# One encoder kernel, one VectorE split moved behind two later steps in the odd layer's head loop

## The reference, cut to what matters

```python
s = einsum('bqhgd,bkhd->bhgqk', qx, kx) * scale     # 128 queries x up to 384 keys
s = where(valid, s, -inf)
m = maximum(max(s), sink)
p = exp(s - m);  p = p / (sum(p) + exp(sink - m))
o = einsum('bhgqk,bkhd->bqhgd', p, vx)
x = x + (o * silu(gate)) @ w_out
```

## Time and profile before

| what | value |
|---|---|
| time, median of 3 runs | 1117.99 us (1117.44 to 1118.64) |
| the profiled execution, its own time | 1119.73 us |
| its span, first to last instruction | 1118.0 us |
| mean granted TensorE clock | 0.994 of full speed |
| PE busy | 1093.4 us, 98% |
| PE weight loads busy | 913.1 us, 82% |
| DVE busy | 967.5 us, 87% |
| ACT busy | 678.7 us, 61% |

### The profile page before, as it was taken

The page is one execution under the profiler, slowest core; times in us unless marked ns, Lnnn a source line. Parts: engine busy times, 40 slices in busy tenths (PEclk is TensorE's granted clock), DMA queues, the critical chain, the costliest instruction groups (busy, mean ns, idle before and its releaser), DMA issues. The chain is left out here.

```text
span 1118.0 us, 18504 instructions
## 1 busy us (share of the span) xinstructions
PE 1093.4 (98%) x5690; PEld 913.1 (82%) x5690; DVE 967.5 (87%) x1956; ACT 678.7 (61%) x1310; POOL 0.2 (0%) x4
## 2 busy tenths in 40 slices
PE   8999999999999999999999999999999999999996
PEld 7778878888888888888888867878888888888876
DVE  6879989889889889889889888888888888988886
ACT  6475665654654654654654765367677666677764
POOL 0000000000000000000000000000000000000000
PEclk9999999999999999999999999999999999999998
DMA  7614423324224224225125120563332324323111
GB/s 231 167 41 106 140 76 93 96 75 101 87 75 114 74 75 125 62 75 140 47 75 150 44 71 22 124 160 97 98 94 56 94 63 121 100 75 94 57 39 76
DMA packets 132634, 103.67 MB, mean 93 GB/s; under 512 B 5488, under 2 KB 118512, under 8 KB 132592
## 3 DMA queue, kind: packets, MB, share of 16 engines
q1 hardware_dynamic: 131760, 102.28, 33.4%
q10 hardware_dynamic: 832, 0.85, 0.2%
HBM read 77.95 MB, written 2.10 MB: 72 GB/s over the span
## 5 line engine op out<-in xcount | busy, mean ns | idle before, releaser
L75 PE MATMUL bank_proj<-hH,w_hi 128*128 128x512 f32 x856 | 341.4, 399 | 1.1 <-DVE w_lo L1323 1.1
L77 PE MATMUL bank_proj<-hH,w_lo 128*128 128x512 f32 x856 | 334.4, 391 | 0.0
L76 PE MATMUL bank_proj<-hL,w_hi 128*128 128x512 f32 x856 | 334.3, 391 | 0.0
L77 PEld LDWEIGHTS bank_proj<-hH,w_lo 128*128 128x128 f32 x856 | 160.8, 188 | 34.9
L75 PEld LDWEIGHTS bank_proj<-hH,w_hi 128*128 128x128 f32 x856 | 161.2, 188 | 32.2 <-DVE w_lo L1323 2.0
L76 PEld LDWEIGHTS bank_proj<-hL,w_hi 128*128 128x128 f32 x856 | 161.2, 188 | 29.8 <-issue 0.2
L2087 ACT ACTIVATE probs<-probs,small 128x256 f32<-128x256 f32 (+1 forms) x128 | 70.9, 556 | 55.2 <-DVE small L2355 54.8
L1323 DVE TENSOR_TENSOR w_lo<-w_raw,w_hi 128x1024 fp32r<-128x1024 f32 x73 | 88.3, 1218 | 0.9 <-ACT w_hi L789 0.9
L2094 ACT ACTIVATE probsT<-bank_odd_turn 128x256 fp32r<-128x256 f32 (+1 forms) x128 | 49.0, 434 | 64.4 <-PE bank_odd_turn L1810 63.7
L789 ACT ACTIVATE w_hi<-w_raw 128x1024 fp32r<-128x1024 f32 x73 | 76.9, 1053 | 0.2
L918 ACT ACTIVATE scaled<-decay 128x1024 f32<-128x1024 f32 x32 | 34.0, 1062 | 61.8 <-PE bank_score L611 59.7
(11 more groups left out here) (463 smaller groups left out, 2157.8 us busy)
## 6 DMA issues: line engine op xcount, KB each, us to landing
w_raw<-in_w_in_even SPq DMA_DIRECT2D x71, 512.0 KB, 4.7
w_raw<-in_w_in_odd SPq DMA_DIRECT2D x36, 512.0 KB, 4.9
qs<-parts SPq DMA_DIRECT2D x96, 128.0 KB, 2.4
ks<-parts SPq DMA_DIRECT2D x40, 256.0 KB, 4.5
o_raw<-in_w_out_even SPq DMA_DIRECT2D x15, 512.0 KB, 6.3
o_raw<-in_w_out_odd SPq DMA_DIRECT2D x14, 512.0 KB, 6.7
mixT<-in_x SPq DMA_DIRECT2D x4, 256.0 KB, 6.0
rope<-in_rope SPq DMA_DIRECT2D x2, 512.0 KB, 7.5
```

The lines of the kernel that those rows point to most:

```text
L75: pe.matmul(out, hi, moving_hi, start=start, stop=False)
L76: pe.matmul(out, hi, moving_lo, start=False, stop=False)
L77: return pe.matmul(out, lo, moving_hi, start=False, stop=stop)
```

## The change

In half 0 of rounds 1 to 7, the split of the next queries (`part(h, 1)`) no longer follows the rotation. The low part of y, the low part of the second transposed block and the maxima of the third block come first, and the split after them. Half 1 keeps its order, and round 0 is as it was. No instruction is added or removed.

```diff
                 if not zeroth:
                     rotate(h, 2 * half + 1)
-                    part(h, 2 * half + 1)
                 if not half and not first:
                     low_y(h - 1, 1)
+                if half:
+                    part(h, 3)
                 low_turn(h, half, 1)
                 maxima(h, half, 2)
+                if not half and not first:
+                    part(h, 1)
                 if first:
                     low(0, 2)
                     part(0, 0)
```

## The result

The changed kernel takes 1119.12 us (median of 21 runs) beside 1116.90 us of the kernel before, timed with it. The medians differ by 2.2 us; the ratio is 1.0015 with a 95% interval of 1.0009 to 1.0021, which is 1.7 us slower, between 1.0 and 2.3. That is less than the 0.2% that the prediction took for the least that can be told from no change, yet the interval excludes 1. The forecast was 1.74 us slower, 1119.7 us by the median of 3 runs shown ahead (1117.99).

What follows compares the result with a forecast made beforehand. TensorE, busy 344.0 of 348 us in the odd layer's loop, was taken as the bound; 0.84 us for six rounds plus 0.90 for round 7 gave +1.74 on 1117.99, 1119.7 us, with a range of 1118.9 to 1120.2 us.

Steps and rivals of the forecast that it cites:

- y's part moves up, the wait goes: Half 0: y's low part starts 0.60 us after the rotation's last addition started; TensorE's 0.32 us wait before `out_tile` 0 goes.
- `low_turn(1)` is held by ScalarE's copy: Half 0, VectorE: `low_turn(1)` starts 1.05 us after `turns(1)`, gaining only 0.40 us, after some 0.8 us idle.
- The split is 1.07 us long and 0.53 us of it are hidden: After the maxima, the split delays VectorE by 1.07 us; the gap before the swapped halves hides 0.53; `low_turn(2)` 0.14 later.
- The upper bound of 1.25 us: The split's longest cost in its new place, both durations end to end plus a 0.13 us gap; +1.3 us over seven rounds.
- Given back at `values(2)`, and 0.14 us on top: Rounds 1 to 6, half 0: TensorE loses the 0.32 us won at `out_tile` 0 plus 0.14 a round, 0.84 us together.
- Round 7 without a gap: Round 7: no idle time hides the split; 1.07 less 0.17 us makes `values(2)` and the tail 0.90 us later.
- The queue costs nothing: SyncE's DMAs behind the split go 3.3 us later, yet queries and weight loads still arrive in time; cost nothing.
- The rival in which the weights come late: Half 1, rounds 1 to 6: load 5 lands too late for ScalarE, costing 4.2 us, 1123.9 us; chance 0.07.
- The rival that ends on the other side, that the gap goes and nothing is given back: TensorE's half 0 goes at half 1's pace, 7.46 us; together -2.6 us, 1115.4 us; chance 0.08.

Runs made afterwards that it cites:

- e3: The changed kernel with half 0's gate scaling moved into VectorE's new idle time ahead of `low_turn(1)`; 1115.42 us, 0.9980 of the kernel before.
- e5: e4 with the second output tile's addition moved behind `low_turn(2)` in all half steps of rounds 1 to 7; 1112.46 us, 0.9952 of the kernel before.
- e1: The kernel before with only y's low part moved ahead of the split in half 0; 1115.76 us, ratio 0.9986 to the kernel before.
- e2: The changed kernel with the split's subtraction done twice in half 0 of rounds 1 to 7; 1123.21 us, 1.0049 of the kernel before.
- e4: e3 with the low parts of weights 3 and 4 moved later in round 7; 1115.04 us, ratio 0.9978 to the kernel before.

## Why the prediction was right, step by step

- *y's part moves up, the wait goes*: in round 2 it started 0.61 us after the rotation's last start (0.60 forecast), and `out_tile` 0 came at 1.35 us. Right.
- *`low_turn(1)` is held by ScalarE's copy*: 820.68 - 819.63 = 1.05 us. Right, and it is why the moved split won so little ahead of it.
- *The split is 1.07 us long and 0.53 us of it are hidden*: it is 1.06 us, the idle gap was used up, and `low_turn(2)` came after 6.82 us (6.84 forecast). The upper bound of 1.25 us did not come: behind the readout of the maxima the copy starts at once.
- *Given back at `values(2)`, and 0.14 us on top*: 7.98 - 7.87 = 0.11 us. Right; half 1 stayed at 7.45 to 7.46. Over rounds 1 to 6, from the first mark to `turns(1)` of round 7, it adds up to 291.93 - 291.08 = 0.85 us (0.84 forecast). That the sum fits so well is partly luck: `values(2)` of half 0 came 0.11 to 0.12 us later in five rounds and 0.18 in round 1, together 0.74, and the last 0.1 us arose elsewhere in these rounds.
- *Round 7 without a gap*: 9.11 - 8.23 = 0.88 us (0.90 forecast), and 0.89 from `turns(1)` to the second mark, since the tail behind `values(2)` took 36.02 us before and 36.03 after. Right.
- *The queue costs nothing*: after the change SyncE's queue, the landing of load 5 (last figure) and ScalarE's two copies, round 2:

```profile
823.87 2.40 SPq L1712 DMA_DIRECT2D qs<-parts  x4
826.65 1.11 SPq L1689 DMA_DIRECT2D w_raw<-in_w_in_odd  x2
```

```profile
w_raw<-in_w_in_odd SPq DMA_DIRECT2D x1, 512.0 KB, 3.9
```

```profile
830.73 2.01 ACT L2074 ACTIVATE w_hi<-w_raw 128x1024 fp32r<-128x1024 f32 x2
```

Load 5 landed at 830.55, about 1.2 us ahead of the second copy if the two copies share their 2.01 us evenly, and this is the time that they took before, too. Right. The rival in which the weights come late did not arise: in rounds 1 to 6 this load landed after 3.9 to 4.1 us. Its limit is off by a tenth in the prediction, where 834.4 - 829.4 is 5.0 and not 5.1 us, so it would have begun at a landing of about 5.5 us.

The rival that ends on the other side, that the gap goes and nothing is given back, failed on its own condition: 1.06 us did not fit into 0.53. It can be had, though: e3 puts the 0.60 us of the gate into the idle time that the change opens, and then `values(2)` comes 0.35 to 0.42 us earlier a round, as that rival had it. The Trainium skill's rule for it (Perfetto Trace Analysis, Optimization Strategy: find the busiest engine's gap and make what releases it start sooner) pointed at the right gap; the runs show that the gain is what the next release on the same engine lets through: of the 0.32 us won at `out_tile` 0 nothing was left at `values(2)`, which came 0.11 us later than before.

## What to carry to other kernels

When instructions of an engine with a fixed order are swapped, add up its chain from the last event that it cannot move (here TensorE's `turns`) to the next place where the bottleneck waits for it, and not only to the wait that is to go. An idle gap on that engine is worth what is put into it: a link moved behind a gap is paid in full less the cover that it finds there, and the time that it vacates is lost unless another link of the same chain fills it. Compare two profiled executions from a mark that neither kernel changes; their spans can have the wrong sign.

## What the runs showed of the hardware that was not expected

Identical code ahead of the change differed by 2.92 us between two executions; 1.22 us of it had arisen by 13 us, where the same multiplication starts at 13.20 us before and at 11.98 after. TensorE in two windows at the start (us, busy, granted clock, DMA share, GB/s), before and after:

```profile
5.00:10.00 5.00, 2.38 (x15) 0.92 1.07 333
10.00:15.00 5.00, 5.00 (x27) 0.74 1.14 328
```

```profile
5.00:10.00 5.00, 3.25 (x21) 1.00 1.03 323
10.00:15.00 5.00, 4.43 (x28) 1.00 1.13 333
```

In the execution of the kernel before, TensorE waited 2.62 us for a piece of its input, and the granted clock fell to its lower level, 1.2 GHz (0.50 from 10 to 12 us); in that of the changed kernel it waited 1.75 us and the clock stayed at 2.4 GHz. The traces of e3 and e5 show the fall too, after waits of 2.23 and 2.67 us; those of e1, e2 and e4 do not, after 1.69, 1.49 and 1.79. In round 7 the wait of 1.60 us after the change, and one of 2.21 us in e2, left the granted clock at 1.00.

A second fall stands in the even layer, and in the same three traces only. TensorE from 655 to 660 us, before and after:

```profile
655.00:660.00 5.00, 5.00 (x24) 0.73 0.01 3
```

```profile
655.00:660.00 5.00, 4.99 (x30) 1.00 0.33 105
```

Just ahead of it TensorE waited twice, 0.92 and 0.78 us before, 0.92 and 0.79 us after, so these two waits alone do not tell the two executions apart. The distance between them grows here from 1.03 us (653.82 against 652.79, the same multiplication) to 2.30 (659.90 against 657.60). Where the remaining 0.6 us arose was not followed up, and neither was what sets off the falls.
